# Mixture-of-experts phase of a hybrid encoder layer: expert sum kept in PSUM, expert weights in one queue

## The chip, the cores and the metric

The kernel runs on one core of a Trainium2 chip. The metric is the device time of one execution in microseconds (us). It is given as the median of several executions of the same program. A profile of one more execution gives the time of every instruction.

## The reference

The layer takes 256 tokens of 1024 channels in float32 and applies three residual sub-layers and a last RMSNorm: a mixing layer (latent attention beside a convolution module), a cross-attention into 256 memory tokens, and a mixture of experts. The change touches the third alone:

```python
logits = t @ w_router + b_router            # t: (256, 1024), 32 experts
top_val, top_idx = top_k(logits, 4); gates = softmax(top_val)
# tokens sorted by expert; for each block of tokens of expert e:
up = xb @ w_up[e] + b_up[e]                 # (tokens, 1024) @ (1024, 2048)
glu = minimum(up[:, :1024], 7.0); lin = clip(up[:, 1024:], -7.0, 7.0)
act = glu * sigmoid(1.702 * glu) * (lin + 1)
y = (act @ w_down[e] + b_down[e]) * gate    # (tokens, 1024) @ (1024, 1024)
out = segment_sum(y, token)                 # then residual, then RMSNorm
```

The weights of one expert are 8 MB (up) and 4 MB (down) in float32. All 32 experts are in use in every execution, so 384 MB of weights pass through the core.

## The kernel before, in words

**Names.** PE is TensorE, DVE is VectorE, ACT is ScalarE, POOL is GpSimd, SP is SyncE. Each engine has a program of its own; they meet at semaphores (`wait_ge`, `then_inc`).

**Weights.** They pass through a ring in SBUF of 20 slabs of 1 MB. An up slab holds 128 rows of an expert's up matrix, a down slab 256 rows of its down matrix. Slabs 8 to 15 hold the up matrix of even experts, 0 to 7 that of odd ones, and 16 to 19 the down matrix of every expert. The 20 slabs are filled ahead during the sub-layers before (`load_up`, `load_down`). After that SP alone issues the loads, in a written order (`replace_up`, `replace_down`): for each expert it waits until PE has used a slab (`up_steps`, `down_steps`) and loads its successor into the same place. It does so in two loops. The first runs over the pairs 0 to 8 (`TURN` = 9), with the up slabs two experts ahead and the down slabs one ahead; then one down matrix is replaced by itself; and a second loop goes over the other pairs, each load at the head of the turn that it belongs to.

**Blocks.** The tokens of an expert are worked on in blocks of up to 64 (`CAP`). An expert with more than 64 tokens has several blocks, and its slabs are replaced after its last one. There are 33 blocks in this execution; they are counted from 0 here. For each block:

1. *Up* (L1478): for each of 8 slabs four matmuls of 512 columns, into bank 0 and 1, in pairs that use one half of the PE columns each. Every float32 matmul is two records in the trace.
2. *Combine* of the block before (`combine`, L1448): the one-hot matrix of that block, transposed and in `PT2`, times its output `y_sb`, gives the expert's share for all 256 tokens, in banks 6, 7, 4 and 5. DVE adds it to the residual stream `xs` in SBUF (`add_up`, L1093), four additions.
3. *Drain*: ACT (L756) and DVE (L1109) copy banks 0 and 1 to `U_sb`, in an order in which the channels are spread with a stride of 8. PE waits for both and transposes it (L1491) into banks 2 and 3.
4. *One-hot*: PE transposes this block's one-hot matrix `P2v` into bank 6 (L1497) and multiplies it with the gates (L1499). ACT copies both (L763, L764).
5. *Activation*: in two halves, DVE adds the bias (L1117), clips (L1121, L1122), multiplies (L1125, L1128); ACT gives the sigmoid (L760). DVE's `add_up` stands ahead of this in its program. After it DVE makes the one-hot matrix of the next block (`onehot`, L1100), from the columns that POOL prepares (L536).
6. *Down* (L1512): four slabs, eight records each, into bank 5. The *gather* of the next block's tokens (`gather`, L1435, the one-hot matrix times `rows`, into bank 4) stands behind the first slab, and `gather_columns` (L1442, transposes into bank 2) ahead of the last. ACT copies each result (L738, L742), and at the end scales the output into `y_sb` (L769).

After the last block comes one more combine and `add_up`; then ACT sums squares (L775), DVE scales (L1136), and SP stores the output.

**Prelude.** The jobs of the sub-layers before take the eight PSUM banks in turn (`bank_of`, `begin`): a job waits until the job eight places before it has left its bank. The router's two jobs, `count`, `rank`, `meta` and `gT` are the last of them; PE waits for DVE's choice of experts (L1043) before `count` (L1420).

Of the kernel before, what the change touches and what calls it, by code (L numbers as in the profile page):

```python
# [6 lines left out]
D = 1024  # L7
T = 256
M = 256
P = 128  # L10
KT = D // P
TT = T // P
# [11 lines left out]
CAP = 64  # L24
# [4 lines left out]
TURN = E // 4 + 1  # L29
# [3 lines left out]
BANK = 512  # L33
# [39 lines left out]
def build_program(nc, x, mem, positions, g_mix, w_in, g_q, w_uq, g_kv, w_ukv, w_dw, b_dw, g_conv_ln,  # L73
# [8 lines left out]
    with ctx:  # L82
# [127 lines left out]
        P2 = buf_v[:, D:D + TT * P]  # L210
        PT2 = wr_sb
        gslot = buf_v[:, D + 256:D + 257]
        G_sb = buf_v[:, D + 288:D + 800]
# [4 lines left out]
        P2v = P2.rearrange("p (a s) -> p a s", a=TT)  # L218

        U_sb = buf_f[:, 0:1024].rearrange("p (j q) -> p j q", j=KT)  # L220
# [5 lines left out]
        COMBINE = (6, 7, 4, 5)  # L226
# [15 lines left out]

        def bank_of(job):
            return banks[job_at[job] % 8]
# [58 lines left out]
        slab_in = [sem(f"slab{i}_in") for i in range(20)]  # L303
        p2_ready = sem("onehot_ready")
# [18 lines left out]
        c_full = sem("combined_full")  # L323
        y_added = sem("y_added")
# [13 lines left out]
        down_v = w_down[0].rearrange("e (p k) n -> e p (k n)", k=KT)  # L338
# [7 lines left out]
        def _(sp):  # L346
# [33 lines left out]
            def load_up(e, base, ks):  # L380
                for k in ks:
                    sp.dma_start(slab(base + k), up_v[e, :, k, :]).then_inc(slab_in[base + k], 16)

            def load_down(e):
                for s in range(4):
                    sp.dma_start(slab(16 + s), down_v[e, :, s * SLAB:(s + 1) * SLAB]).then_inc(slab_in[16 + s], 16)
# [3 lines left out]
            load_up(0, 8, (0, 1, 2, 3, 7))  # L390
# [3 lines left out]
            load_up(1, 0, range(4, 8))  # L394
            wait_drained(sp, "xs11")
            load_up(0, 8, [4])
            wait_drained(sp, "xv3")
            load_up(1, 0, range(0, 4))
            wait_drained(sp, "xo3")
            sp.dma_start(gffn, g_ffn[0:1, :].broadcast_to([P, D])).then_inc(loaded["gffn"], 16)  # L400
            load_up(0, 8, (5, 6))
# [4 lines left out]
            load_down(0)  # L406
# [11 lines left out]
            def replace_up(e, n, base):  # L418

                for k in range(KT):  # L420
                    sp.wait_ge(up_steps, n * KT + (k + 1))
                    load_up(e, base, [k])

            def replace_down(e, n):
                for s in range(4):
                    sp.wait_ge(down_steps, n * 4 + (s + 1))
                    sp.dma_start(slab(16 + s), down_v[e, :, s * SLAB:(s + 1) * SLAB]).then_inc(slab_in[16 + s], 16)

            with sp.Fori(0, TURN) as pair:
                e = pair * 2  # L430
                n = last_block(e)
                replace_up(e + 2, n, 8)
                replace_down(e + 1, n)
                n = last_block(e + 1)
                replace_up(e + 3, n, 0)
                replace_down(e + 2, n)


            replace_down(2 * TURN + 1, last_block(2 * TURN))
            with sp.Fori(TURN + 1, E // 2) as pair:  # L440
                e = pair * 2
                n = last_block(e - 1)
                replace_up(e, last_block(e - 2), 8)
                replace_down(e, n)
                replace_up(e + 1, n, 0)
                replace_down(e + 1, last_block(e))
            for a in range(TT):
                sp.wait_ge(fin_ready, a + 1)
                sp.dma_start(out[0, a * P:(a + 1) * P, :], xs[:, a, :]).then_inc(stored, 16)
# [1093 lines left out]
```

## Time and profile before

| | before |
|---|---|
| median of 3 runs | 1319.62 us (1318.1 to 1319.63) |
| profiled execution, span from first to last instruction | 1316.5 us |
| PE busy | 1190.1 us |
| DVE busy | 403.3 us |
| ACT busy | 264.7 us |
| DMA, mean over the span | 331 GB/s, 435.90 MB |
| first up matmul of block 0 | 287.91 us from the span's start |

The profiled execution has its span alone on record: it is 3.1 us shorter than the median of the runs. The start and end of a program lie around the span and are in the runs' time. Busy time of PE is not PE at its peak, since matmuls overlap and their ends are modelled. The granted clock is a share of TensorE's full 2.4 GHz; 0.50 is 1.2 GHz. The DMA share is the mean busy share of the core's 16 DMA engines.

### The profile page before, as it was taken

To read this page: it belongs to the slowest core of one execution; us is meant where nothing else is said; L and a number is where in the kernel's file an instruction comes from. 1 tells how busy PE (TensorE), PEld (TensorE's weight loads), DVE (VectorE), ACT (ScalarE), POOL (GpSimd) and SP (SyncE) were. 2 spreads that over 40 slices of the span, in tenths; PEclk is the share of its full clock that TensorE was granted. 3 is DMA by queue.
4 is the path that set the end of the run, shared out by engine and by line. 5 is a ranking of instruction groups with operands and counts; after the bars stand their busy time and mean duration, and the time that the engine had idled before them with its cause. 6 is when DMAs were issued, how large, how long until landed. Compare 5 with 4: busy or idle time off the path is not lost.

```text
span 1316.5 us, 17217 instructions
## 1 busy us (share of the span) xinstructions
PE 1190.1 (90%) x5298; PEld 516.2 (39%) x5299; DVE 403.3 (31%) x896; ACT 264.7 (20%) x453; POOL 85.7 (7%) x204
## 2 busy tenths in 40 slices
PE   6969999979999989999999999999899999999996
PEld 5748457533333333333333333333333333333332
DVE  1389523042222333222222222223332222222224
ACT  2223111121112112111112111121121111121112
POOL 1195000010000000000000000000000000000000
PEclk9989999969999999999999999999999999999998
DMA  9232474549999999999289999977999999999980
GB/s 359 91 105 90 166 285 161 208 182 382 407 415 407 411 412 409 411 411 409 98 339 402 408 412 411 409 295 267 415 405 409 417 406 410 407 403 417 404 354 32
DMA packets 73183, 435.90 MB, mean 331 GB/s; under 512 B 16227, under 2 KB 16398, under 8 KB 24014
## 3 DMA queue, kind: packets, MB, share of 16 engines
q1 hardware_dynamic: 73166, 435.68, 82.4%
q8 instruction: 10, 0.16, 0.0%
q14 instruction: 7, 0.06, 0.0%
HBM read 434.61 MB, written 1.05 MB: 331 GB/s over the span
## 4 chain that ended last, share of the span: by engine, by line
PE 79%; DVE 13%; issue 5%; ACT 1%; DVEq 0%; DMA 0%; SPq 0%; ACTq 0%
PE bank L1478 35%; PE bank L1512 22%; PE bank L1435 5%; DVE buf_x L1093 4%; PE bank L1190 2%; PE bank L1363 2%; PE bank L1212 2%; PE bank L1402 2%; PE bank L1442 2%; DVE buf_f L1117 2%; DVE ring L903 1%; DVE buf_f L1125 1%; DVE buf_m L1128 1%; PE bank L1313 1%; PE bank L1203 1%
## 5 line engine op out<-in xcount | busy, mean ns | idle before, releaser
L1478 PE MATMUL bank<-ring,buf_m 128*64 128x512 f32 x2112 | 461.0, 594 | 1.1 <-ACT buf_m L742 1.1
L1512 PE MATMUL bank<-ring,buf_m 128*64 128x512 f32 x1056 | 297.1, 702 | 79.5 <-DVE buf_m L1128 79.5
L1478 PEld LDWEIGHTS bank<-ring,buf_m 128*64 128x64 f32 x2112 | 152.2, 138 | 304.0 <-issue 304.0
L1109 DVE COPY buf_f<-bank 128x512 f32<-128x512 f32 x33 | 43.0, 1302 | 685.1 <-PE bank L1478 685.1
L1512 PEld LDWEIGHTS bank<-ring,buf_m 128*64 128x64 f32 x1056 | 79.4, 157 | 222.5 <-issue 222.5
L756 ACT ACTIVATE buf_f<-bank 128x512 f32<-128x512 f32 x33 | 43.5, 1319 | 350.8 <-PE bank L1478 350.8
L1093 DVE TENSOR_TENSOR buf_x<-bank,buf_x 128x512 f32<-128x512 f32 x136 | 85.4, 699 | 10.7 <-PE bank L1448 10.7
L1448 PE MATMUL bank<-buf_m,wr_sb 64*128 64x512 f32 x272 | 67.6, 615 | 0.9 <-ACT buf_m L769 0.9
L1435 PE MATMUL bank<-buf_k,buf_v 128*64 128x512 f32 x272 | 65.9, 606 | 0.9 <-DVE buf_v L1062 0.9
L536 POOL TENSOR_TENSOR buf_v<-table,buf_v 128x4 f32<-128x4 f32 x33 | 6.6, 199 | 905.4 <-PE bank L1499 905.2
L760 ACT ACTIVATE buf_m<-buf_f 128x256 f32<-128x256 f32 x66 | 27.5, 416 | 163.6 <-DVE buf_f L1121 163.6
L753 ACT ACT_TABLE_LOAD x33 | 42.3, 1283 | 33.9 <-issue 33.8
L1117 DVE TENSOR_TENSOR buf_f<-bank,buf_v 128x512 f32<-128x512 f32 x66 | 45.4, 688 | 0.0
L1435 PEld LDWEIGHTS bank<-buf_k,buf_v 128*64 128x64 f32 x272 | 23.0, 162 | 56.1 <-issue 35.9
L738 ACT ACTIVATE buf_v<-bank 128x512 f32<-128x512 f32 x34 | 20.3, 597 | 120.5 <-PE bank L1435 120.5
L903 DVE SCALAR_TENSOR_TENSOR ring<-ring,taps 128x256 f32<-128x256 f32 x90 | 43.8, 565 | 0.0
L742 ACT ACTIVATE buf_m<-bank 128x512 f32<-128x512 f32 x34 | 20.3, 597 | 113.9 <-PE bank L1442 113.9
L1448 PEld LDWEIGHTS bank<-buf_m,wr_sb 64*128 64x128 f32 x272 | 23.4, 186 | 44.5 <-issue 44.5
L1491 PEld LDWEIGHTS bank<-ident,buf_f 128*128 128x128 f32 x264 | 28.3, 141 | 25.0 <-ACT buf_f L756 25.0
L1491 PE MATMUL bank<-ident,buf_f 128*128 128x128 f32 x264 | 36.1, 280 | 0.0
L1203 PE MATMUL bank<-buf_m,ring 128*128 128x256 f32 x128 | 29.6, 394 | 2.5 <-ACT buf_m L609 2.5
L769 ACT ACTIVATE buf_m<-bank,buf_v 128x512 f32<-128x512 f32 x33 | 22.7, 687 | 42.3 <-PE bank L1512 42.3
(273 smaller groups left out, 876.4 us busy)
## 6 DMA issues: line engine op xcount, KB each, us to landing
ring<-in_w_up_dram SPq DMA_DIRECT2D x256, 1024.0 KB, 11.2
ring<-in_w_down_dram SPq DMA_DIRECT2D x128, 1024.0 KB, 6.8
ring<-in_w_in_dram SPq DMA_DIRECT2D x4, 1440.0 KB, 11.0
ring<-in_w_xkv_dram SPq DMA_DIRECT2D x2, 2048.0 KB, 24.3
ring<-in_w_xkv_dram SPq DMA_DIRECT2D x1, 4096.0 KB, 13.1
ring<-in_w_out_dram SPq DMA_DIRECT2D x1, 4096.0 KB, 14.0
ring<-in_w_xq_dram SPq DMA_DIRECT2D x2, 2048.0 KB, 21.0
ring<-in_w_xo_dram SPq DMA_DIRECT2D x1, 4096.0 KB, 12.9
```

The source lines that it names most:

```text
L753: a.activation(scrap[:, 3:4], eps[:, 0:1], ACT.Sigmoid)
L756: a.activation(U_sb[:, :, 0:64].rearrange("p j q -> p q j"), banks[0][:, :].rearrange("p (q j) -> p q j", j=KT), ACT.Copy).then_inc(u_by_a, 1)
L903: ins = v.scalar_tensor_tensor(acc[:, c, :], src, wt, acc[:, c, :], ALU.mult, ALU.add)
L1093: v.tensor_tensor(s, banks[COMBINE[2 * t + n]][:, :], s, ALU.add).then_inc(y_added, 1)
L1109: v.tensor_copy(U_sb[:, :, 64:128].rearrange("p j q -> p q j"), banks[1][:, :].rearrange("p (q j) -> p q j", j=KT)).then_inc(u_by_v, 1)
L1117: v.tensor_tensor(A_sb[:, js], banks[2 + i][:, :].rearrange("p (j h t) -> p j h t", j=4, h=2), bias, ALU.add).then_inc(biased, 1)
L1203: ins = t_.matmul(b[:, j * M:(j + 1) * M], wk_sb[:, k, at:at + P], mT[:, k, :], start=k == 0, stop=k == KT - 1)
L1435: ins = t_.matmul(banks[4][h * 64:(h + 1) * 64, :], P2v[:, a, h * 64:(h + 1) * 64], rows[:, a, 4 * h:4 * h + 4, :], start=a == 0, stop=a == 1)
L1448: t_.matmul(banks[COMBINE[2 * a + h]][:, :], PT2[h * 64:(h + 1) * 64, a * P:(a + 1) * P], y_sb[h * 64:(h + 1) * 64, :], start=True, stop=T ...
L1478: ins = t_.matmul(banks[c][h * 64:(h + 1) * 64, :], xg[:, k, :], w[:, h * FF + c * BANK:h * FF + (c + 1) * BANK], start=k == 0, stop=k == ...
L1491: ins = t_.transpose(banks[2 + j // 4][:, (j % 4) * P:(j % 4 + 1) * P], U_sb[:, j, :], ident[:, :])
L1512: ins = t_.matmul(banks[5][h * 64:(h + 1) * 64, :], actT[:, j, :], w[:, h * BANK:(h + 1) * BANK], start=j == 0, stop=j == KT - 1)
```

## The change

All of it lies in the expert phase and the few jobs ahead of it.

- **Sum in PSUM.** Banks 4 to 7 become the running sum of the layer (`acc2`). Four matmuls with the identity put the residual stream into them before `count`; each combine adds to them (`start=False`). `add_up` is gone. The last norm reads PSUM.
- **Banks.** The last ten jobs of the prelude and all else of the expert phase share banks 0 to 3.
- **One queue of slabs.** Slab number `at` (12 for each expert, 8 up and 4 down, in the order of use) goes to slot `at % 20`. SP loads in that order, and waits for the slab 20 places before. The PE loop is written out for five experts (`CYCLE`), 60 slabs, after which the slots repeat.
- **Order on PE.** The one-hot transposes and the gather of the next block come ahead of the down slabs. `gather_columns` comes between the two halves of them. The transposes of the first half wait for ACT's drain alone.
- **Second one-hot.** DVE makes the one-hot matrix twice: for the gather (`P2v`, one block ahead) and for the combine (`P2bv`, in `buf_x`), both at the start of a block, ahead of its wait for the up slabs.
- **Layout.** The host hands `w_down` and `b_up` over in another order. A down slab is still 8 KB in one piece for each partition. The drain of `U_sb` becomes a plain copy, and the bias is one load of 2 KB rows instead of two of 32-byte pieces.

```diff
-TURN = E // 4 + 1
+RING, SLABS, CYCLE = 20, 12, 5
...
-        banks = [ctx.enter_context(nc.psum_tensor(f"bank{i}", [P, BANK], fp32)) for i in range(8)]
+        low_banks = [ctx.enter_context(nc.psum_tensor(f"bank{i}", [P, BANK], fp32)) for i in range(4)]
+        acc2 = [ctx.enter_context(nc.psum_tensor(f"total{t}", [P, D], fp32)) for t in range(TT)]
...
+        bank_no = [i % 8 if i < FIRST_LOW else (i - FIRST_LOW) % 4 for i in range(len(JOBS))]
...
-            bup_v = b_up[0].rearrange("e (h p j) -> p e h j", h=2, j=KT)
-            for h in range(2):
-                sp.dma_start(bup4[:, :, h, :], bup_v[:, :, h, :]).then_inc(loaded["bup"], 16)
+            sp.dma_start(bup_sb[:, :], b_up).then_inc(loaded["bup"], 16)
...
+            n1 = last_block(0)
+            for i in range(4):
+                sp.wait_ge(up_steps, n1 * KT + (i + 1))
+                load_down(1, SLABS, i)
+            with sp.Fori(0, (E - 2) // CYCLE) as turn:
+                for j in range(2, 2 + CYCLE):
+                    e = turn * CYCLE + j
+                    n2 = last_block(e - 2)
+                    for k in range(4):
+                        sp.wait_ge(up_steps, n2 * KT + (k + 5))
+                        load_up(e, j * SLABS, k)
+                    for k in range(4, KT):
+                        sp.wait_ge(down_steps, n2 * 4 + (k - 3))
+                        load_up(e, j * SLABS, k)
+                    n1 = last_block(e - 1)
+                    for i in range(4):
+                        sp.wait_ge(up_steps, n1 * KT + (i + 1))
+                        load_down(e, j * SLABS, i)
...
@@ POOL @@
-                    pool.wait_ge(pt_full, b + 1)
+                    pool.wait_ge(p2b_ready, b * 3 + 1)
...
@@ ACT @@
-                    a.activation(U_sb[:, :, 0:64].rearrange("p j q -> p q j"),
-                                 banks[0][:, :].rearrange("p (q j) -> p q j", j=KT), ACT.Copy).then_inc(u_by_a, 1)
-                    for i in range(2):
-                        act.wait_ge(glu_ready, b * 2 + (i + 1))
-                        a.activation(sig[:, 4 * i:4 * i + 4, :], A_sb[:, 4 * i:4 * i + 4, 0, :], ACT.Sigmoid,
-                                     scale=ALPHA).then_inc(sig_ready, 1)
+                    a.activation(U_sb[:, 0:BANK], banks[0], ACT.Copy).then_inc(u_by_a, 1)
+                    act.wait_ge(glu_ready, b * 2 + 1)
+                    a.activation(sig[:, 0:4, :], A_sb[:, 0:4, 0, :], ACT.Sigmoid, scale=ALPHA).then_inc(sig_ready, 1)
                     act.wait_ge(pt_full, b + 2)
-                    a.activation(PT2[:, :], banks[6][:, 0:T], ACT.Copy)
-                    a.activation(gslot, banks[6][:, T:T + 1], ACT.Copy).then_inc(pt_copied, 1)
-                    gathered(b + 1)
-                    gathered_columns(b + 1)
+                    a.activation(PT2[:, :], banks[0][:, 0:T], ACT.Copy)
+                    a.activation(gslot, banks[0][:, T:T + 1], ACT.Copy).then_inc(pt_copied, 1)
+                    act.wait_ge(glu_ready, b * 2 + 2)
+                    a.activation(sig[:, 4:8, :], A_sb[:, 4:8, 0, :], ACT.Sigmoid, scale=ALPHA).then_inc(sig_ready, 1)
+                    gathered(b + 1, 1)
+                    gathered_columns(b + 1, 0)
...
@@ DVE @@
+                    onehot_for_combine(b)
+                    onehot_for_gather(b + 1)
                     dve.wait_ge(up_steps, b * KT + KT)
-                    v.tensor_copy(U_sb[:, :, 64:128].rearrange("p j q -> p q j"),
-                                  banks[1][:, :].rearrange("p (q j) -> p q j", j=KT)).then_inc(u_by_v, 1)
-                    add_up(b)
+                    v.tensor_copy(U_sb[:, BANK:2 * BANK], banks[1]).then_inc(u_by_v, 1)
...
@@ PE @@
+            for t in range(TT):
+                for n in range(2):
+                    t_.matmul(banks[4 + 2 * t + n], ident[:, :], xs[:, t, n * BANK:(n + 1) * BANK], start=True, stop=False)
...
+                    pe.wait_ge(xg_ready, n + 1)
+                    up_slabs(n, turn, j)
+                    pe.wait_ge(y_ready, n + 1)
+                    pe.wait_ge(pt_copied, n + 1)
+                    combine()
+                    pe.wait_ge(u_by_a, n + 1)
+                    for f in range(4):
+                        ins = t_.transpose(banks[2][:, f * P:(f + 1) * P], U_sb[:, f * P:(f + 1) * P], ident[:, :])
+                    ins.then_inc(t_full, 1)
+                    pe.wait_ge(u_by_v, n + 1)
+                    for f in range(4, KT):
+                        ins = t_.transpose(banks[3][:, (f - 4) * P:(f - 3) * P], U_sb[:, f * P:(f + 1) * P], ident[:, :])
+                    ins.then_inc(t_full, 1)
+                    pe.wait_ge(p2b_ready, n * 3 + 4)
+                    for a in range(TT):
+                        t_.transpose(banks[0][:, a * P:(a + 1) * P], P2bv[:, a, :], ident[:, :])
+                    for a in range(TT):
+                        ins = t_.matmul(banks[0][:, T:T + 1], P2bv[:, a, :], gcol[:, a:a + 1], start=a == 0, stop=a == 1)
+                    ins.then_inc(pt_full, 1)
+                    gather(n + 1, 1)
+                    down_slabs(n, turn, j, 0)
+                    pe.wait_ge(pt_copied, n + 2)
+                    gather_columns(n + 1, 0)
+                    down_slabs(n, turn, j, 1)
```

## Rows read from the trace of the kernel before

**Rows 1.** The page: busy time of PE, DMA share and GB/s in 40 slices.

```profile
PE 1190.1 (90%) x5298; PEld 516.2 (39%) x5299; DVE 403.3 (31%) x896; ACT 264.7 (20%) x453; POOL 85.7 (7%) x204
...
DMA  9232474549999999999289999977999999999980
GB/s 359 91 105 90 166 285 161 208 182 382 407 415 407 411 412 409 411 411 409 98 339 402 408 412 411 409 295 267 415 405 409 417 406 410 407 403 417 404 354 32
```

**Rows 2.** The chain of waits from 474.4 to 505.1: start, duration, what.

```profile
474.35 13.76 PE bank L1478 x64
...
491.74 0.61 DVE buf_f L1117
...
493.99 3.47 PE bank L1512 x8
497.46 1.72 PE bank L1435 x8
499.18 3.43 PE bank L1512 x16
```

**Rows 3.** The timeline of the same block: start, duration, instruction, idle before and releaser.

```profile
488.01 1.99 PE L1448 MATMUL bank<-buf_m,wr_sb 64*128 64x512 f32 x8
489.93 1.09 PE L1491 MATMUL bank<-ident,buf_f 128*128 128x128 f32 x8
493.99 3.47 PE L1512 MATMUL bank<-ring,buf_m 128*64 128x512 f32 x8 [2.41 <-DVE buf_m L1128]
...
489.24 2.50 DVE L1093 TENSOR_TENSOR buf_x<-bank,buf_x 128x512 f32<-128x512 f32 x4
491.67 0.67 DVE L1117 TENSOR_TENSOR buf_f<-bank,buf_v 128x512 f32<-128x512 f32 x1
...
499.23 0.60 ACT L738 ACTIVATE buf_v<-bank 128x512 f32<-128x512 f32 x1 [3.66 <-PE bank L1435]
```

**Rows 4.** Windows: length, busy PE, PEld, DVE, ACT, POOL, clock, DMA share, GB/s.

```profile
474.35:505.07 30.72, 28.31 (x132) 10.37 (x130) 8.07 (x18) 5.85 (x10) 0.60 (x3) 0.94 1.01 412
627.95:658.70 30.75, 28.34 (x132) 10.37 (x130) 7.90 (x17) 5.85 (x10) 0.59 (x3) 0.94 0.20 73
873.70:904.42 30.72, 28.30 (x133) 10.37 (x130) 8.08 (x18) 5.86 (x10) 0.60 (x3) 0.94 0.39 145
...
603.00:619.00 16.00, 13.58 (x66) 5.47 (x64) 7.65 (x17) 2.48 (x5) 0.40 (x2) 0.92 1.01 426
...
362.00:380.00 18.00, 15.60 (x73) 6.01 (x70) 8.07 (x18) 3.06 (x6) 0.60 (x3) 0.91 1.01 421
...
482.35:484.35 2.00, 2.00 (x12) 0.70 (x10) 0.00 (x0) 0.00 (x0) 0.00 (x0) 1.00 1.03 434
```

**Rows 5.** Windows around PE's wait, and one of an earlier sub-layer, same columns.

```profile
494.35:497.35 3.00, 3.00 (x10) 0.79 (x8) 1.85 (x7) 0.75 (x3) 0.00 (x0) 0.54 1.02 423
...
98.00:103.00 5.00, 4.12 (x24) 2.82 (x24) 5.00 (x9) 4.12 (x8) 4.75 (x7) 1.00 0.00 0
```

**Rows 6.** The timeline from the last sub-layer to block 0.

```profile
257.68 8.75 PE L1402 MATMUL bank<-ring,buf_m 128*128 128x512 f32 x20
...
277.22 0.27 PE L1420 MATMUL bank<-ones,buf_m 128*32 128x1 f32 x2 [4.76 <-DVE buf_m L1043]
...
287.91 16.12 PE L1478 MATMUL bank<-ring,buf_m 128*64 128x512 f32 x64 [1.08 <-ACT buf_m L742]
...
291.78 12.77 SPq L382 DMA_DIRECT2D ring<-in_w_up_dram  x8
```

**Rows 7.** Up loads issued between 350 and 700 (86 of them): issue to landing.

```profile
DMA to landing us min/median/max: 4.7/10.4/13.8
```

**Rows 8.** The timeline of the tail.

```profile
1301.85 1.94 PE L1512 MATMUL bank<-ring,buf_m 128*64 128x512 f32 x8
...
1305.82 2.48 DVE L1093 TENSOR_TENSOR buf_x<-bank,buf_x 128x512 f32<-128x512 f32 x4 [10.73 <-PE bank L1448]
1306.50 0.20 ACT L772 ACTIVATE scrap<-eps 128x1 f32<-128x1 f32 x1
1307.15 1.06 ACT L775 ACTIVATE buf_f<-buf_x 128x1024 f32<-128x1024 f32 x1 [0.45 <-DVE buf_x L1093]
```

More of the change, by code:

```diff
@@ L241, in build_program @@
         NDRAIN = {s: sum(1 for j in JOBS if j[2] == s) for s in "va"}
+        FIRST_LOW = job_at["tT00"]
+        bank_no = [i % 8 if i < FIRST_LOW else (i - FIRST_LOW) % 4 for i in range(len(JOBS))]
         def bank_of(job):
-            return banks[job_at[job] % 8]
+            return banks[bank_no[job_at[job]]]
         def wait_full(eng, job):
@@ L299, in build_program @@
         table_ready = sem("ranks_and_gates_in_table")
-        slab_in = [sem(f"slab{i}_in") for i in range(20)]
-        p2_ready = sem("onehot_ready")
+        slab_in = [sem(f"slab{i}_in") for i in range(RING)]
+        p2_ready = sem("onehot_for_gather_ready")
+        p2b_ready = sem("onehot_for_combine_ready")
         pt_full = sem("transposed_onehot_full")
@@ L405, in _ @@
                 sp.dma_start(y_sb[h * 64:h * 64 + E, :], b_down[0, :, h * BANK:(h + 1) * BANK]).then_inc(loaded["bdown"], 16)
-            load_down(0)
+            for k in range(4, KT):
+                load_up(1, SLABS, k)
             sp.wait_ge(rows_ready, TT)
@@ L1146, in begin @@
                 i = job_at[job]
-                if i >= 8:
-                    wait_drained(pe, JOBS[i - 8][0])
+                same = [j for j in range(i) if bank_no[j] == bank_no[i]]
+                if same:
+                    wait_drained(pe, JOBS[same[-1]][0])
                 return bank_of(job)
@@ new lines, in up_slabs @@
+            def up_slabs(n, turn, j):
+                for k in range(KT):
+                    at = j * SLABS + k
+                    pe.wait_ge(slab_in[slot_of(at)], turn * (CYCLE * SLABS // RING * 16) + (at // RING + 1) * 16)
+                    w = slab(slot_of(at))
+                    for c in range(2):
+                        for h in range(2):
+                            ins = t_.matmul(banks[c][h * 64:(h + 1) * 64, :], xg[:, k, :],
+                                            w[:, h * FF + c * BANK:h * FF + (c + 1) * BANK],
+                                            start=k == 0, stop=k == KT - 1)
+                    ins.then_inc(up_steps, 1)
@@ new lines, in down_slabs @@
+            def down_slabs(n, turn, j, half):
+                pe.wait_ge(act_ready, n * 2 + (half + 1))
+                for i in (2 * half, 2 * half + 1):
+                    at = j * SLABS + KT + i
+                    pe.wait_ge(slab_in[slot_of(at)], turn * (CYCLE * SLABS // RING * 16) + (at // RING + 1) * 16)
+                    for k in range(2):
+                        f = 2 * i + k
+                        for h in range(2):
+                            ins = t_.matmul(banks[2][h * 64:(h + 1) * 64, :], actT[:, f, :],
+                                            slab(slot_of(at))[:, k * D + h * BANK:k * D + (h + 1) * BANK],
+                                            start=f == 0, stop=f == KT - 1)
+                    ins.then_inc(down_steps, 1)
@@ new lines, in expert @@
+            def expert(e, turn, j):
+                extra = pe.value_load(meta_i[0:1, bass.ds(e, 1)], min_val=0, max_val=T // CAP - 1)
+                first = pe.value_load(meta_i[0:1, bass.ds(e + E, 1)], min_val=0, max_val=E + T * TOPK // CAP)
+                with pe.Fori(0, pe.snap(extra + 1)) as r:
+                    n = pe.snap(first + r)
+                    pe.wait_ge(xg_ready, n + 1)
[22 more added lines that the diff above has]
+                    down_slabs(n, turn, j, 1)
@@ L1516, in _ @@
+            with pe.Fori(0, E // CYCLE) as turn:
+                for j in range(CYCLE):
+                    expert(turn * CYCLE + j, turn, j)
+            for e in range(E - E % CYCLE, E):
+                expert(e, E // CYCLE, e % CYCLE)
             last_b = pe.value_load(meta_i[0:1, 2 * E - 1:2 * E], min_val=0, max_val=E + T * TOPK // CAP)
@@ L1519, in _ @@
             pe.wait_ge(y_ready, blocks + 1)
-            pe.wait_ge(y_added, blocks * 4 + 1)
-            combine()
+            pe.wait_ge(pt_copied, blocks + 1)
+            combine(last=True)
 _INS = ['x', 'mem', 'positions', 'g_mix', 'w_in', 'g_q', 'w_uq', 'g_kv', 'w_ukv', 'w_dw', 'b_dw', 'g_conv_ln',
```

192 lines of the change are left out of this document (65 added, 127 removed).

## The prediction

> **What bounds the kernel now.** I read the page first: PE is 90% busy, and the row of DMA shares stands at 9 through most of the last three quarters, with a dip to 98 and 339 GB/s in slices 20 and 21 and a smaller one later [rows 1]. Two resources look full, so the page alone can't say which one sets the time. The chain of waits over one block decides it [rows 2]: eight up slabs 13.76 us, then a stretch that runs through VectorE, then the down slabs. It has no DMA piece at all, and the PE idle in the timeline of the same block is one wait of 2.41 us before L1512, released by VectorE's L1128 [rows 3]. The windows confirm it from the other side [rows 4]: the block from 474.35 moves 412 GB/s at a share of 1.01, the blocks from 627.95 and 873.70 move 73 and 145 GB/s, and all three take 30.72 to 30.75 us with the same PE busy time. Starving the transfers for most of a block changed nothing, so weights always arrive in time and PE sets the period: 33 blocks (32 experts, one of them with two) at 30.72 us. The DMA share says only that PE's demand (12 slabs of 1.0486 MB, 12.58 MB in 30.72 us, 410 GB/s) lies close under what the engines carry.
>
> How close? In two stretches with loads queued up the rate is 426 and 421 GB/s [rows 4]: 2.46 and 2.49 us a slab, I take 2.48, so 29.8 us for an expert. PE's 30.72 is 0.96 us above that. This is the number on which the forecast hangs: anything saved on PE beyond 0.96 us a block runs into the transfers.
>
> **PE's part, step by step.** By its timeline [rows 3] PE ends its transposes and the gate column at 491.58 and waits for the activation until 493.99. The first down slab then takes 3.47 us for eight records, where L1435's eight take 1.72 and sixteen of L1512 take 3.43 [rows 2]. The granted clock over 494.35 to 497.35 is 0.54, the lower of the two levels, 1.2 GHz [rows 5]; before it PE had narrow transposes and then the wait.
> - The gather of the next block (1.72 us) moves from behind the first down slab into that wait. L1117 starts at 491.67 today, held by the four residual additions (L1093, until 491.74). Without them it can start when the first four transposes are in, about 490.55; the activation is then ready 2.3 us later (L1117's start to PE's start in rows 3), at 492.9. The gather fills PE from 491.6 to 493.3. The wait goes: -2.41 us.
> - With no idle the clock should hold, and the first down slab takes 1.73: -1.74 us.
> - The strided drain of U becomes contiguous, from 1.3 to about 0.6 us (L738 has that size and takes 0.60). It lies beside the combine (1.99 us) before and after: 0. If that cover went, it would cost PE its 0.6.
> - The combine adds in PSUM instead of overwriting. Same instructions and columns; 0, bounded by 0.5 either way, a quarter of its row. The second one-hot, its copy and POOL's columns, all small, move to the top of the block under the up phase, 13.8 us long: 0.
> PE's block: 30.72 - 2.41 - 1.74 = 26.57 us. 33 of them from 287.9, plus 2.4 for the first one's low clock (16.12 us for its up slabs instead of 13.76 [rows 6]), end at 1167.
>
> **The transfers' part.** Of 384 slabs 20 are loaded ahead, as before, and 364 follow. Now they form one queue in order of use, each freed by the slab 20 places before it. The two dips go: they came from the order (a down load waiting ahead of up loads whose slots were free; a doubled expert holding its slots). The doubled expert is number 10 from zero: in its second block, number 11 from 627.95, nothing can be replaced. Its first slab (120) lands near 544, PE starts it at 556, and releases the slot in the second pass at about 584; slab 140 could start at 592. Its down slots come free 8 us before they are due. So a queue of 20 bridges the doubled expert, by some 5 us after the issue's own latency. The first follow-up load is issued at 291.8 [rows 6], lands 4.7 us later, the shortest time to landing seen [rows 7], and 363 more at 2.48 take 900.2: the last slab lands at 1196.7.
>
> That is 30 us later than PE could be done, so **the bound changes from PE to the transfers**. PE meets them near the twentieth expert and then waits about 0.8 us in front of some slabs. The last slab is a down slab. The last up slab is 9.9 us before it; behind that PE has 1.7 + 5.3 (combine, transposes, gather) + 6.9 + 0.6 = 14.5 us, so PE ends 4.6 us after the last landing, at 1201.3.
>
> **The tail.** Now 12.7 us from the last down matmul (1303.8) to the span's end. The four additions (L1093, from 1305.82) go, and ScalarE's square starts when the sum is in PSUM; but it stands behind a table load that ends at 1306.7, so only 0.4 us of its 1307.15 start is gained [rows 8]. The two squares and the last scaling read PSUM instead of SBUF: 0, within 0.5. Tail 12.3: the span ends at 1213.6.
>
> **The prelude.** Four identity matmuls put the residual into the accumulator: 0.87 us each at full clock (20 records in 8.75), 3.5 us together. They lie in PE's wait of 4.76 us for the routing [rows 6]. If the clock has already fallen there they take 7.0 and push the routing by 2.2. In return a PE kept busy may reach the first block at the higher clock, which frees its first slots 1.7 us sooner. From -1.7 to +2.2; I take +1. Banks 0 to 3 are reused after four jobs instead of eight; each such wait is on a job already waited for: 0. The bias load's short rows ran where nobody waits for them: 0.
>
> Sum: span 1214.6. The profiled span is 1316.5 and the median of the runs 1319.6, so 3.1 lie around it: **1218 us**.
>
> Two rules of the Trainium skill bear on the rate. DMA: Bandwidth & Descriptors (section Bandwidth) gives a ceiling of about 435 GB/s; at it the sum would come to some 1192 (an estimate from that page), and the peak window here, 434 GB/s, agrees with it as a peak. The same section names about 358 GB/s as a core's share of the memory, which would leave nothing to gain from this change; the rows above 410 GB/s speak against it for a core alone.
>
> **The rivals.**
> - *PE stays the bound*, because the lower clock still comes once a block (the narrow transposes remain, only the idle goes): 28.31 us a block, 287.9 + 2.4 + 934.2 + 12.3 + 3.1 = 1240. A residual wait of 1.7 us gives the same. Against: with the gather in place there is no idle left in the stretch. 13%.
> - *The transfers carry only their average of today*, 410 GB/s, 2.56 us a slab: 363 x 0.08 = 29 more, 1247. For: the share already reads 1.00. Against: the stretches of 421 to 426 GB/s beside it. 8%.
> - *A queue that never runs dry is faster*: at the peak window's 434 GB/s, 2.416 us, 23 less: 1195. 5%.
> - *Slower than before*: waits of 0.8 us before slabs pull the clock down, and PE then loses more than it saved. Place: the up phase of each block. Price: half of each microsecond at 1.2 GHz. It decides from 8.5 us of low clock a block (26.57 + 4.25 = 30.8); at 12 us a block lasts 32.6 and the kernel 1381. For: one idle of 2.4 us costs the clock today. Against: in 98 to 103 PE is idle for 0.88 of 5 us at clock 1.00 [rows 5], and a PE slower than the transfers has no waits left to lower its clock. 4%. (The Trainium skill, TensorE: Matmul & The Clock Gate, HAM oscillation, tells of a thin matmul kernel that is throttled again at each slice it waits for; this is that case if the waits are long enough, and no row here shows it for short ones.)
> - *Nothing gained*: another wait, such as the pause for the transposed one-hot before the gather's columns, takes the place of the one removed. 2%.
>
> **How the numbers follow.** The forecast case has 68%, from 1210 to 1226 by its own bounds. The range 1200 to 1248 adds the first two rivals and part of the third. Within 0.2% (2.6 us), about what a measurement of this kernel can tell from no change: 2%. Slower 4%, faster 94%.
>
> **What would show it.** Right: the down slabs no longer wait for VectorE; the first down slab takes 1.7 us; blocks of 26.6 us until about expert 20, then 29.8 us with PE waits on DMA of the ring; a DMA row of 9s without dips at 421 to 426 GB/s; last slab landing near 1197. Wrong: PE idle on VectorE in each block, a clock below 1.00 once a block, blocks other than 26.6 early on, or a rate under 415 GB/s with all slots queued.

## The result and the profile after

| | before | after |
|---|---|---|
| median of the runs | 1319.44 us (4 runs, 1318.1 to 1319.63) | 1234.78 us (4 runs, 1234.07 to 1236.51) |
| ratio to before | | 0.9365 [0.9353, 0.9376] |
| profiled span | 1316.5 us | 1232.4 us |
| PE busy | 1190.1 us | 1152.1 us |
| packets on queue q14, kind "instruction" | 7 | 33 |

The change takes 84.7 us off. The forecast was 1218, so the kernel is 17 us slower than forecast: inside the range of 1200 to 1248, but outside the 1210 to 1226 that the forecast case gave itself. The page after, with the busy row, the DMA rows over 40 slices and the queues (packets, MB, share of 16 engines); it answers to [rows 1]:

```profile
PE 1152.1 (93%) x5306; PEld 497.6 (40%) x5307; DVE 330.0 (27%) x859; ACT 237.0 (19%) x453; POOL 85.7 (7%) x204
...
DMA  9230643909999999999999999999999999999991
GB/s 354 93 145 3 271 171 137 370 22 394 422 421 421 421 422 422 421 421 422 421 422 422 421 422 422 421 422 421 421 404 422 421 422 422 391 422 422 421 398 46
...
q1 hardware_dynamic: 65086, 435.68, 85.7%
q8 instruction: 16, 0.26, 0.1%
q14 instruction: 33, 0.27, 0.1%
```

The two dips of before are gone and the rate stands at 421 to 422. Yet three late slices read 404, 391 and 398, and the last row is one that the prediction didn't reckon with: q14, which carries instructions, has 33 packets.

**One block.** The timeline after, the stretch of [rows 3]:

```profile
514.28 1.99 PE L1449 MATMUL total<-buf_m,wr_sb 64*128 64x512 f32 x8
516.20 0.66 PE L1510 MATMUL bank<-ident,buf_f 128*128 128x128 f32 x4
...
516.90 0.69 DVE L1117 TENSOR_TENSOR buf_f<-bank,buf_v 128x512 f32<-128x512 f32 x1 [1.80 <-PE bank L1510]
...
517.79 1.94 PE L1436 MATMUL bank<-buf_k,buf_v 128*64 128x512 f32 x8
...
518.68 0.42 DVE L1128 TENSOR_TENSOR buf_m<-buf_f,buf_m 128x256 f32<-128x256 f32 x1
...
519.55 3.60 PE L1490 MATMUL bank<-ring,buf_m 128*64 128x512 f32 x16
...
523.67 3.65 PE L1490 MATMUL bank<-ring,buf_m 128*64 128x512 f32 x16
```

No idle stands before L1490, the down slabs. VectorE's last piece (518.68 to 519.10) ends while PE is in the gather, L1436. Sixteen down records take 3.60 us from the first on; in [rows 3] the first eight alone took 3.47.

**Blocks along the way.** Windows of an early block, of the expert with two blocks, of a late block, and of the stretch from 340 to 1190 (length, busy PE, PEld, DVE, ACT, POOL, clock, DMA share, GB/s), as in [rows 4]:

```profile
500.45:527.16 26.71, 26.71 (x133) 9.96 (x130) 5.93 (x17) 5.01 (x10) 0.60 (x3) 1.00 1.01 422
580.50:612.00 31.50, 27.82 (x132) 9.52 (x130) 5.75 (x16) 5.02 (x10) 0.60 (x3) 1.00 1.01 421
1081.50:1111.30 29.80, 27.10 (x128) 9.22 (x126) 5.92 (x17) 5.02 (x10) 0.60 (x3) 1.00 1.01 422
...
340.00:1190.00 850.00, 813.48 (x3898) 292.89 (x3896) 177.50 (x509) 150.49 (x300) 17.13 (x86) 1.00 1.01 420
```

A block is 26.7 us with PE full. It meets the transfers once, in block 11 (31.5 us, the first pass of the doubled expert), gets ahead again in the second pass, and from block 20 on lasts 29.8 and at times 30.5 to 32. The clock is 1.00 throughout. The waits behind this (us in all, times, longest):

```profile
PE bank L1476 <- DMA ring<-in_w_up_dram: 38.5, 61, 1.3
```

**The last 25 us of the weights**, same columns as the windows above:

```profile
1190.00:1195.00 5.00, 5.00 (x26) 1.72 (x24) 0.00 (x0) 2.17 (x3) 0.00 (x0) 1.00 1.01 421
1195.00:1200.00 5.00, 4.45 (x22) 1.11 (x18) 0.00 (x0) 0.00 (x0) 0.00 (x0) 1.00 0.95 397
1200.00:1205.00 5.00, 3.97 (x20) 0.97 (x16) 0.00 (x0) 0.00 (x0) 0.00 (x0) 1.00 0.07 31
1205.00:1210.00 5.00, 4.47 (x21) 1.47 (x20) 0.69 (x1) 0.60 (x1) 0.00 (x0) 1.00 0.06 26
1210.00:1215.00 5.00, 5.00 (x32) 2.62 (x32) 3.98 (x10) 1.65 (x5) 0.00 (x0) 1.00 0.08 31
```

This is the lesson of the whole profile. From 1200 on the share is 0.06 to 0.08, about a sixteenth: one of the 16 DMA engines works alone for some 15 us (from 1202 on the trace has one weight packet at a time under way), while the others have nothing left and PE still waits for slabs (3.97 busy of 5). A slab is complete when its slowest engine is done. Mean rate and mean share hide that, since both are full until the others finish.

**What SP does meanwhile.** The queue's loads come from a loop written out for five experts. The chain of SP at the jump back to the head of that loop (start, us, what):

```profile
1035.86 1.93 SPq L394
...
1037.97 5.39 issue
1043.36 0.06 SPq L436
...
1043.98 4.09 issue
...
1048.15 0.06 SPq L429
```

Two pauses of 5.39 and 4.09 us in which nothing that the profile shows was waited for: SP fetches its own instructions, over the DMA engines that carry the weights. In the trace q14 packets start at 1041.7 and 1046.4, and each pause ends 1.3 to 1.4 us after the end of one. In the list of landings the usual slab lands 2.486 us after its predecessor (median of 363), but 28 of them come over 0.4 us later than that, most after 3.2. The mean is 2.539, and 363 x 0.053 = 19.2 us are what the late ones cost; 26 packets more than before by some 0.72 us are 18.7. The packets themselves tie the two together. From 431 us on 25 packets of q14 come, and behind each of them, within 3.4 us, one slab lands late, by 0.5 to 0.8 us; no other slab is late there. Such a packet of 8 KB takes 0.31 us, as long as one of weights, and the weight packet that starts at its end takes 0.72 instead of 0.31. Together these are the 0.72 us (0.31 + 0.41). The pauses cost nothing beyond that. The window behind them, columns as above, shows why:

```profile
1045.00:1050.00 5.00, 3.20 (x16) 0.80 (x14) 0.00 (x0) 0.00 (x0) 0.00 (x0) 1.00 0.66 272
```

The share falls to 0.66, as the engines that are ahead run out of loads; but the slabs of these microseconds still complete 2.5 to 3.2 us apart, by the engine that is behind and has work. That was the theory taken to the chip (A): **each instruction fetch delays the one DMA engine that carries it, and through it the queue**. Its rival (B): the doubled expert and the order of the queue cost the time, or the engines carry no more than this. The transfers' bound itself had to be shown too.

### The profile page after: what moved, and what is told of

It reads as the page before. It is cut to its first block, busy times and chain, and to the rows that moved or that the text cites. A ratio compares the mean times of both kernels' runs of the same rounds, so it can differ in the third digit from the quotient of the medians.

```text
span 1232.4 us, 17087 instructions
## 1 busy us (share of the span) xinstructions
PE 1152.1 (93%) x5306; PEld 497.6 (40%) x5307; DVE 330.0 (27%) x859; ACT 237.0 (19%) x453; POOL 85.7 (7%) x204
## 4 chain that ended last, share of the span: by engine, by line
PE 47%; SPq 36%; issue 6%; DMA 5%; DVE 3%; ACT 2%; ACTq 0%; DVEq 0%
SPq L390 22%; PE bank L1476 14%; SPq L394 11%; PE bank L1490 8%; DMA ring<-in_w_up_dram 5%; PE total L1449 2%; PE bank L1436 2%; PE bank L1188 2%; PE bank L1361 2%; PE bank L1210 2%; DVE ring L903 1%; SPq L429 1%; SPq L428 1%; PE bank L1201 1%; PE total L1400 1%
## 5 line engine op out<-in xcount | busy, mean ns | idle before, releaser
L1476 PE MATMUL bank<-ring,buf_m 128*64 128x512 f32 x2112 | 474.1, 597 | 40.3 <-DMA ring<-in_w_up_dram 38.5
L1490 PE MATMUL bank<-ring,buf_m 128*64 128x512 f32 x1056 | 239.5, 595 | 0.0
L1111 DVE COPY buf_f<-bank 128x512 f32<-128x512 f32 x33 | 22.8, 692 | 589.9 <-PE bank L1476 589.9
L1490 PEld LDWEIGHTS bank<-ring,buf_m 128*64 128x64 f32 x1056 | 72.8, 136 | 137.6 <-issue 129.2
L759 ACT ACTIVATE buf_f<-bank 128x512 f32<-128x512 f32 x33 | 19.7, 597 | 403.3 <-PE bank L1476 403.3
L1449 PE MATMUL total<-buf_m,wr_sb 64*128 64x512 f32 x272 | 67.6, 615 | 0.8 <-ACT buf_m L771 0.8
L1436 PE MATMUL bank<-buf_k,buf_v 128*64 128x512 f32 x272 | 65.9, 605 | 0.7 <-DVE buf_v L1062 0.7
L1449 PEld LDWEIGHTS total<-buf_m,wr_sb 64*128 64x128 f32 x272 | 23.4, 186 | 44.5 <-issue 42.8
L505 POOL TENSOR_SCALAR buf_f<-ring,taps 128x256 f32<-128x256 f32 x30 | 30.0, 1000 | 0.0
L1125 DVE SCALAR_TENSOR_TENSOR buf_f<-buf_f 128x256 f32<-128x256 f32 x66 | 28.1, 425 | 6.9
L1128 DVE TENSOR_TENSOR buf_m<-buf_f,buf_m 128x256 f32<-128x256 f32 x66 | 28.1, 425 | 2.3
L1443 PEld LDWEIGHTS bank<-ident,buf_v 128*128 128x128 f32 x136 | 14.2, 140 | 28.2 <-issue 28.2
L509 POOL TENSOR_TENSOR ring<-ring,buf_f 128x256 f32<-128x256 f32 x30 | 25.0, 833 | 2.5
L1436 PEld LDWEIGHTS bank<-buf_k,buf_v 128*64 128x64 f32 x272 | 16.6, 136 | 20.7 <-issue 20.2
```

The lines of the kernel that those rows point to most:

```text
L505: g.tensor_scalar(prod, src, wt, None, ALU.mult).then_inc(conv_prod_ready, 1)
L1125: v.scalar_tensor_tensor(lin, lin, 1.0, glu, ALU.add, ALU.mult).then_inc(prod_ready, 1)
L1128: v.tensor_tensor(actT[:, js, :], lin, sig[:, js, :], ALU.mult).then_inc(act_ready, 1)
L1436: ins = t_.matmul(banks[bank][h * 64:(h + 1) * 64, :], P2v[:, a, h * 64:(h + 1) * 64], rows[:, a, 4 * h:4 * h + 4, :], start=a == 0, stop= ...
L1449: ins = t_.matmul(banks[4 + 2 * a + h], PT2[h * 64:(h + 1) * 64, a * P:(a + 1) * P], y_sb[h * 64:(h + 1) * 64, :], start=False, stop=last)
L1476: ins = t_.matmul(banks[c][h * 64:(h + 1) * 64, :], xg[:, k, :], w[:, h * FF + c * BANK:h * FF + (c + 1) * BANK], start=k == 0, stop=k == ...
```

## The experiments

The diffs are against the changed kernel, unless said otherwise.

**Loads in pairs (e1).** Half as many load instructions, each of 2 MB, into two neighbouring slots; SP's loop is shorter.

```diff
-                    for k in range(4):
-                        sp.wait_ge(up_steps, n2 * KT + (k + 5))
-                        load_up(e, j * SLABS, k)
+                    for k in (0, 2):
+                        sp.wait_ge(up_steps, n2 * KT + (k + 6))
+                        load_up2(e, j * SLABS, k)
```

> The changed kernel with SP's loads behind the first 20 slabs issued two slabs at a time (2 MB), so that SP's loop has half as many instructions. Theory A (SP's loop over five experts is too long for its instruction store, is fetched again each turn in blocks of 8 KB over the same DMA engines, and each fetch makes one slab land 0.7 us late): the about 24 fetches after 400 us mostly vanish, the mean from one slab to the next goes from 2.54 to about 2.49 us, 363 x 0.05 = 18 us less, minus 2.5 us at the end for the coarser last load: 1218 to 1222 us. Rival B (the late slabs come from something in the memory or in the deep queue, not from the program's length): spikes stay, 1235 to 1238 us.

Measured: 1216.74 us (1215.72 to 1220.73), 0.9237 [0.9213, 0.9261] of before, 18.0 us under the changed kernel. The row of the instruction queue on e1's page:

```profile
q14 instruction: 7, 0.06, 0.0%
```

e1's windows at the end, and over the long stretch:

```profile
1190.00:1195.00 5.00, 5.00 (x30) 2.60 (x28) 1.88 (x4) 0.83 (x2) 0.00 (x0) 1.00 0.98 416
1195.00:1200.00 5.00, 5.00 (x25) 1.53 (x22) 2.80 (x7) 1.42 (x5) 0.00 (x0) 1.00 0.14 56
...
340.00:1190.00 850.00, 822.22 (x3976) 302.03 (x3974) 178.08 (x511) 153.22 (x304) 17.82 (x89) 1.00 1.01 424
```

The packets are back at 7, the lone engine's last stretch is gone, and the last pair lands at 1197.3, about where the other 15 engines had finished in the changed kernel. The size of a load isn't what helps: a pair takes 4.965 us (median), 2.483 a slab, as before. The time is 1.3 us under A's 1218 to 1222 and 18 us from B's: the direction and size are A's.

**The loop unrolled (e2).** Same loads of 1 MB, same waits, but SP never jumps back; its whole program is read once.

```diff
-            with sp.Fori(0, (E - 2) // CYCLE) as turn:
+            for turn in range((E - 2) // CYCLE):
```

> The changed kernel with SP's loop over the turns written out in full (30 experts in a row, no jump back). Theory A (fetches of SP's program cost the slabs): the pauses of 4 to 5 us of SP at the jump back vanish; every instruction is fetched once, about 12 to 15 blocks of 8 KB instead of 24, so 7 to 9 us less: 1226 to 1229 us. If only the jump back fetches: under 1222 us. Rival B (not the program): 1235 us.

Measured: 1221.89 us (1221.24 to 1222.54), 0.9268 [0.9253, 0.9284]. The same row on e2's page, and behind it a window at e2's end:

```profile
q14 instruction: 14, 0.11, 0.0%
```

```profile
1200.00:1205.00 5.00, 5.00 (x24) 1.43 (x20) 2.88 (x8) 1.57 (x5) 0.00 (x0) 1.00 0.05 20
```

This run is the cleanest of the set, as nothing but the fetching differs: 19 packets fewer, 12.9 us less, 0.68 each. A's 1226 to 1229 was missed on the low side, since more packets vanished than the 9 to 12 that it reckoned with. The changed kernel's trace has the two pauses at each of its five jumps back; e2's has none of them. The Trainium skill (Runtime: NRT & Kernel Launch, Instruction fetch mechanics) says that a jump to a place outside the two pages held forces a fetch before execution goes on, and that this is a reason to unroll. The chain above and e2 agree with it. That fetching in sequence is hidden, as the same section has it, holds here for SP, whose queue of loads outlasts its pauses, but not for the transfers beside it.

**More instructions in the loop (e8).** Fifty waits that are always met, for each expert.

```diff
                     n2 = last_block(e - 2)
+                    for i in range(50):
+                        sp.wait_ge(const_ready, 1)
```

> The changed kernel with 50 waits more for each expert in SP's loop, on a semaphore that has long been reached, so that the loop has about twice as many instructions and does the same. Theory A (each fetch of SP's program makes a slab late by 0.7 us): the fetches after 340 us grow from 31 to some 55, 24 x 0.72 = 17 us more: 1248 to 1256 us. Rival B (the gains of the shorter loops came from their loads or from the missing jump, not from the volume fetched): 1235 us.

Measured: 1242.68 us (1241.18 to 1245.07), 0.9428 [0.941, 0.9446]; 7.9 us slower. The same row on e8's page, and behind it e8's long window:

```profile
q14 instruction: 39, 0.32, 0.1%
```

```profile
340.00:1190.00 850.00, 809.66 (x3876) 290.61 (x3874) 174.37 (x500) 149.18 (x298) 17.34 (x88) 1.00 1.00 417
```

The direction is A's: no load and no wait that could bite was added, yet the transfers slowed. The expected number missed, because only 6 more packets came and not 24; so how many packets a longer loop brings can't be worked out from its length. The 7.9 us aren't all the price of these 6. The last landing is 7.6 us later than in the changed kernel; by the list of landings 0.7 of it stand before the first follow-up slab (the first behind the 20 loaded ahead), 3.0 arise between there and 340 us, while the queue fills, and 3.9 behind 340, where 5 more packets stand: 0.8 us each, near the 0.7 of e2.

**Half of every load (e3).** The follow-up loads bring the first 1024 of 2048 columns of each slab.

```diff
+                sp.dma_start(slab(slot)[:, 0:D], up_v[e, :, k, 0:D]).then_inc(slab_in[slot], 16)
```

> The changed kernel, but from the third expert on only the first half of each slab is loaded (4 KB of each partition's 8 KB); the rest of the slab keeps what was there, so the products are of other numbers and the time of PE is the same. Theory A (the transfers set the time from about expert 20 on, PE's block alone takes 26.7 us): PE never waits for a slab, 285.4 + 28.1 + 32 x 26.71 = 1168, with the tail 11.6 and 2.4 around the span 1182 us. Rival (PE has waits of its own that the transfers only cover): blocks stay near 28 to 29 us, above 1215 us.

Measured: 1183.93 us (one run), as expected. The windows of a block and of a long stretch of e3:

```profile
500.00:526.70 26.70, 26.70 (x134) 9.96 (x131) 5.92 (x17) 5.01 (x11) 0.60 (x3) 1.00 0.71 236
...
340.00:1150.00 810.00, 810.00 (x3944) 301.95 (x3942) 177.82 (x511) 152.72 (x303) 17.43 (x88) 1.00 0.66 222
```

With the transfers out of the way PE is busy in every one of 810 us. So the transfers are the bound of the changed kernel, and 51 us lie between it and PE's own time.

**The old order of loads under the new PE program (e4).** SP's section, the preloads and the places of the slabs of before.

```diff
-RING, SLABS, CYCLE = 20, 12, 5
+RING, SLABS, CYCLE = 20, 12, 2
+TURN = E // 4 + 1
...
+            with sp.Fori(0, TURN) as pair:
+                e = pair * 2
+                n = last_block(e)
+                replace_up(e + 2, n, 8)
+                replace_down(e + 1, n)
...
```

> The changed kernel on PE, ACT, DVE and POOL, with SP's old order of loads and the old places of the slabs (two loops, pairs of experts). Theory A (the two dips of the DMA row were free only because PE was slower): the dips stay in the trace (about 25 us in the block of the doubled expert, 19 + 4 us at the change of loops) and are no longer covered; the short loop bodies of SP bring no fetches. Transfers 1235 - 18 + 47 less PE's slack of some 15: about 1250, between 1238 and 1268 us. Rival (the order of the loads doesn't matter, the gain is all in the order on PE): 1215 to 1235 us.

Measured: 1224.77 us (1224.14 to 1225.59), 0.9292 [0.9276, 0.9307]. **My theory missed by 25 us**, and the rival's bounds held: the order that I had blamed for the dips is 10 us *faster* than the new queue. e4's page, the 40 slices and the instruction queue:

```profile
GB/s 353 103 141 1 275 172 138 350 45 342 420 422 422 422 421 422 422 422 422 421 307 423 421 422 422 422 422 422 423 421 421 423 421 423 421 422 422 422 422 210
...
q14 instruction: 7, 0.06, 0.0%
```

PE's waits for up slabs in e4 (us, times, longest):

```profile
PE bank L1482 <- DMA ring<-in_w_up_dram: 16.5, 30, 0.6
```

And e4's window of the doubled expert:

```profile
606.00:633.00 27.00, 24.98 (x120) 8.98 (x118) 5.75 (x16) 5.02 (x10) 0.60 (x3) 1.00 0.72 291
```

One dip is left, at a share of 0.72: 27 x 0.28 = 7.6 us lost. The one at the change of loops is gone. The traces have three kernels with this same order of loads and a faster and faster PE. The longest times between two landings are 30.2 and 20.7 us before the change (blocks of 30.7 us), 17.5 and 12.3 in e7 below (28.9), and 8.8 and no second one here (26.7 until the transfers set the time). So the dips measured how far ahead the transfers were, with every slot full, and not what the order costs once they are the bound.

**The new queue alone in the kernel before (e5).** Against the kernel before; SP's section of the change, and PE's slab numbers to match.

```diff
+                    for k in range(4):
+                        sp.wait_ge(up_steps, n2 * KT + (k + 5))
+                        load_up(e, j * SLABS, k)
...
```

> The kernel before, with the new queue of 20 slabs in order of use alone (PE's loop over five experts); all else as before. Theory A (PE's order sets 30.72 us a block, weights always came in time): 1319 us, within 2 us, with a DMA row without dips until the ring is full and a share below 1 later. Rival (the old order cost time): 1290 us or less.

Measured: 1318.06 us (10 runs, 1316.96 to 1320.2), 1.0003 [0.9993, 1.0012] of before. e5's page, and behind it its long window:

```profile
PE 1192.3 (91%) x5298; PEld 515.2 (39%) x5299; DVE 403.2 (31%) x896; ACT 264.8 (20%) x453; POOL 85.7 (7%) x204
...
GB/s 358 101 96 100 157 287 162 206 197 377 405 417 404 393 393 422 422 421 364 147 340 401 416 409 372 422 421 422 370 412 422 422 421 369 423 422 421 421 95 32
...
q14 instruction: 33, 0.27, 0.1%
```

```profile
340.00:1190.00 850.00, 786.79 (x3602) 285.45 (x3600) 219.64 (x493) 162.10 (x278) 15.87 (x80) 0.94 0.95 394
```

All 33 fetches are there and cost nothing, since PE is the bound. The time is A's, the row is not: the dip of the doubled expert is there with the new order too (147 and 340 GB/s; 27.1 us between two landings, 30.2 before), and only the second dip, at the change of loops, is gone (at most 5.2 us between landings there). So the first dip didn't come from the order of loads. That is why a trial of the queue by itself would have shown neither its gain nor its fault.

**The gather back behind the first down slabs (e6).** One run.

```diff
-                    gather(n + 1, 1)
 
                     down_slabs(n, turn, j, 0)
+                    gather(n + 1, 1)
                     pe.wait_ge(pt_copied, n + 2)
                     gather_columns(n + 1, 0)
```

> The changed kernel with the gather put back behind the first half of the down slabs. Theory A: PE waits again for the activation, from 517.85 to about 519.3 in the block that starts at 500.45, so 1.4 us; if the clock falls as it did before the change, 1.7 us more. Block 28.1 us without and 29.8 us with the fall of the clock; the transfers still take 29.8 us and more, so the kernel's time moves little: 1235 to 1240 us without, 1265 to 1275 us with the fall, since PE then has no lead. Rival (the wait before the down slabs was made by the additions alone and is gone with them): block 26.7 us, 1235 us.

Measured: 1260.14 us, a block 28.9, in neither of the two expected bands. The timeline of a block of e6, and behind it the window around the wait:

```profile
513.31 3.65 PE L1490 MATMUL bank<-ring,buf_m 128*64 128x512 f32 x16 [1.30 <-DVE buf_m L1128]
...
516.79 1.89 PE L1436 MATMUL bank<-buf_k,buf_v 128*64 128x512 f32 x8
```

```profile
510.00:516.00 6.00, 4.70 (x30) 2.55 (x30) 3.98 (x10) 1.17 (x4) 0.00 (x0) 1.00 1.01 421
```

The wait for the activation is back at 1.30 us, and the clock stays at 1.00. The other 0.79 us are a wait that neither case foresaw, of `gather_columns` (L1443) for ScalarE's copy of the gather (L741). 26.7 + 1.3 + 0.8 = 28.8. PE sets the time again. The run is 25 us longer, but its block 0 starts at 290.53 instead of 285.43, behind sub-layers that the edit leaves alone; from block 0 on the two differ by 20.9 us. So the place of the gather is worth some 21 us in this kernel, and only part of that by the wait that the change was described with.

**The additions shrunk (e7).** Against the kernel before: `add_up` works on one column of 512. One run.

```diff
-                        s = xs[:, t, n * BANK:(n + 1) * BANK]
-                        v.tensor_tensor(s, banks[COMBINE[2 * t + n]][:, :], s, ALU.add).then_inc(y_added, 1)
+                        s = xs[:, t, n * BANK:n * BANK + 1]
+                        v.tensor_tensor(s, banks[COMBINE[2 * t + n]][:, 0:1], s, ALU.add).then_inc(y_added, 1)
```

> The kernel before with the four additions of the experts' shares cut to one column of 512 each (the rest of the sum is left out). Theory A (the additions held the bias step back by 1.2 us): PE's wait falls from 2.41 to 1.2 to 1.3 us, 33 x 1.15 = 38 us less: 1281 us, and 57 us more (1225 us) if the shorter wait also keeps the clock up. Rival (the additions lie beside the transposes anyway): 1319 us.

Measured: 1260.31 us, a block 28.9, between the two cases. The timeline of a block of e7, and behind it its window:

```profile
514.17 1.94 PE L1512 MATMUL bank<-ring,buf_m 128*64 128x512 f32 x8 [1.38 <-DVE buf_m L1128]
...
516.60 1.94 PE L1435 MATMUL bank<-buf_k,buf_v 128*64 128x512 f32 x8 [0.50 <-DVE buf_v L1100]
```

```profile
512.00:517.00 5.00, 3.12 (x19) 1.39 (x18) 4.20 (x12) 1.17 (x4) 0.70 (x3) 1.00 1.01 423
```

DVE's share of the old wait of 2.41 us [rows 3] was 1.03. With 1.38 us of idle the clock holds and the first eight down records take 1.94 us instead of 3.47. Then a wait that the late down slab had covered comes up, 0.50 us for the next one-hot (L1100). So 1.5 us of the old block came from the lower clock behind the long idle, while 1.38 us of idle at the same place cost no clock. Block 0 starts at 291.74 here and at 287.91 before, so from there on the gain is 61.7 us, and not the 57.6 between the times.

**Pairs, with the first four down slabs one at a time (e9).** Against e1, to start the queue earlier.

```diff
-            for i in (0, 2):
-                sp.wait_ge(up_steps, n1 * KT + (i + 2))
-                load_down2(1, SLABS, i)
+            for i in range(4):
+                sp.wait_ge(up_steps, n1 * KT + (i + 1))
...
```

> The version with two slabs a load, but with the four down slabs of the second expert, the first loads behind the 20, issued one at a time as in the changed kernel. Expected: the first of them is issued one slab (1.7 to 3.4 us) sooner, the transfers start sooner by as much, and since they set the end it comes 2 to 3 us sooner: 1213 to 1215 us. Rival (the start doesn't matter, because PE has 20 slabs ahead): 1217 us.

Measured: 1218.51 us (1216.58 to 1222.56), 0.925 [0.923, 0.927], no gain over e1 that can be told. The first follow-up load is issued 4.5 us earlier (289.0 instead of 293.5), the last lands 0.9 us earlier (1196.4). Most of the lead is lost at once: the tenth follow-up slab lands at 321.0, and in e1 at 321.5. SP issues nothing between 302.3 and 311.1 (e1: between 304.0 and 312.8), since the next load waits until PE has used the first down slabs of block 0. At the start PE still sets the pace of the queue.

The runs with 1 MB or 2 MB loads, side by side:

| kernel | q14 packets | last landing | median |
|---|---|---|---|
| e1, pairs | 7 | 1197.3 | 1216.74 |
| e4, old order (7.6 us of gap) | 7 | 1207.3 | 1224.77 |
| e2, unrolled | 14 | 1204.2 | 1221.89 |
| changed kernel | 33 | 1215.7 | 1234.78 |
| e8, padded | 39 | 1223.3 | 1242.68 |

## Why the prediction was right and where it failed

**Right.** The wait for the activation and the low clock of the first down slab both went; the block is 26.71 us against 26.57. The bound moved to the transfers, PE first waits for them late, and they run without dips. A slab's usual step is 2.486 us against 2.48. PE ends 5.1 us after the last landing against 4.6; the tail is 11.6 us against 12.3.

**The prelude** was better than +1. The identity matmuls ran from the lower clock (0.50 in 272 to 274) into the higher (1.00 in 276 to 278), in 5.17 us where the prediction had 3.5 or 7.0, and the gather of block 0 behind them took 1.94 us instead of 3.68. The timeline after, at the stretch of [rows 6]:

```profile
271.47 5.17 PE L1417 MATMUL total<-buf_x,ident 128*128 128x512 f32 x8
276.57 0.22 PE L1421 MATMUL bank<-ones,buf_m 128*32 128x1 f32 x2
...
285.43 15.28 PE L1476 MATMUL bank<-ring,buf_m 128*64 128x512 f32 x64 [1.68 <-issue]
```

Block 0 starts at 285.43 instead of 287.91 and its up slabs take 15.28 us instead of 16.12. The second of these may be luck of this one execution: in six others with the same prelude (e1 to e4, e8, e9) block 0 starts at 285.2 to 286.8 and its up slabs take 16.9 to 17.0. With the earlier issue the first follow-up slab lands at 294.1 where 296.5 was forecast.

**The step that failed** is the term "363 more at 2.48 take 900.2". It took 921.6 (294.1 to 1215.7), 21.4 us more, a mean step of 2.539. The price of a slab was right; what was missing is a second user of the DMA engines, the instruction fetches of SP. The other terms gave back 2.4 - 0.5 + 0.7 + 1.0 = 3.6, which leaves 17.8 of the span (1232.4 against 1214.6), and around the span lay 2.4 instead of 3.1. The 3.1 was never a cost around the span alone: each run on record is 1.6 to 1.8 us longer than its own span, and the rest is how far the profiled execution was from the median. e1, the same queue without the extra fetches, came to 1216.7 against the forecast 1218. The rival of a lower carrying rate (2.56 us a slab) came near the measured mean of 2.539, but for a reason of its own, most of which one line of code removed (e2). That the measured time lies inside the stated range is in part luck: the upper part of the range was there for this rival and for a PE that stays the bound, and neither came.

**Also wrong.** Which expert is doubled: it is number 11 from zero, with blocks 11 and 12. The block from 627.95 in [rows 4], number 11, is its first pass, not its second, and it is the first pass that frees nothing: SP issues no load between 628.5 and 660.6, where block 12 has begun. PE met the transfers in block 11 already, and not only near the twentieth expert. And "the two dips go: they came from the order" holds for the second dip alone: e5 keeps the first with the new order. It also gave the order a worth that it doesn't have: e4 shows 7.6 us for the doubled expert and nothing for the change of loops.

**The slower rival** (waits before slabs pull the clock down) didn't come: 61 waits of 0.6 us on average, 1.3 at most, at a clock of 1.00.

**Where the gain comes from**, by the runs (beside them the kernel before took 1317.9 to 1318.5): the PE, DVE and ACT side under the old order takes 93 us (e4: 1317.9 to 1224.8); the new queue alone 0 (e5); the queue as written costs 10 on top (e4 to after); the same queue without its fetches gains 8 (e4 to e1). How the 93 divide is shown, by one run each, for the gather's place alone (25, or 21 from block 0 on, e6) and for DVE's additions in the old kernel (58, e7: 1317.9 to 1260.3, or 62 from block 0 on); the two overlap and aren't to be added. The best of the kernels is **e1 with 1216.74 us**, ahead of both; e9 can't be told from it.

## What to carry to other kernels

When an engine's loop issues transfers that fill the DMA engines, its instructions are traffic on the same engines: look at the instruction queues in the page, keep the loop body short, and issue fewer and larger loads. A dip in the transfer rate while another engine sets the time shows how far ahead the transfers are; don't book its area as a gain for the time when they become the bound. Try a queue and an engine program each without the other: here one gave nothing alone, the other gave more than both together.

## What the hardware showed that I had not expected

- Instruction fetches on q14 came in packets of 8 KB (33 packets, 0.27 MB), and each cost the queue of weights some 0.7 us where it was measured cleanly (e2). The packet itself took 0.31 us, like one of weights; the other 0.41 us lie in the weight packet behind it, which took 0.72. Why that one is slow wasn't tried.
- The delay falls on a single DMA engine of the 16 and adds up over the kernel, to 15 us at share 0.06 to 0.08 at the end.
- The longer idle cost the clock and the shorter ones didn't: behind 2.41 us in front of the down slabs it was 0.54 [rows 3, 5], behind 1.30 and 1.38 us at the same place (e6, e7) 1.00.
- One core alone drew 424 GB/s over 850 us (e1). No run here had a second core at work, so what two would get isn't shown.
